# The up weights of the last two experts, issued in ScalarE's DMA queue instead of SyncE's

## What is computed

```python
hid = (jax.nn.silu(jnp.einsum('bld,edh->bleh', xf, w_gate[grp]))
       * jnp.einsum('bld,edh->bleh', xf, w_up[grp]))
y = y + jnp.einsum('bleh,ble,ehd->bld', hid, combine[:, :, grp], w_down[grp])
```

## Time and profile before

| what | value |
|---|---|
| time, median of 3 runs | 1054.71 us (1054.44 to 1054.72) |
| time of the profiled execution | 1053.88 us |
| its span, first to last instruction | 1052.1 us |
| TensorE busy | 1010.9 us, 96% |
| mean granted TensorE clock | 0.986 of full speed |
| HBM read and written | 169.16 MB, 12.60 MB |

### The profile page before, as it was taken

How to read it: one execution, slowest core, us unless ns; L and a number is a source line. 1 busy time by engine, 2 the same in 40 slices (tenths; PEclk the granted TensorE clock), 3 DMA queues, 4 the chain that set the end, 5 groups by cost and what they waited for, 6 DMA issues and landing times. The chain is left out here.

```text
span 1052.1 us, 20893 instructions
## 1 busy us (share of the span) xinstructions
PE 1010.9 (96%) x8969; PEld 719.1 (68%) x8969; DVE 575.6 (55%) x1114; ACT 312.1 (30%) x581; POOL 112.6 (11%) x109
## 2 busy tenths in 40 slices
PE   9999999999999999999999999999999999787897
PEld 8888888877787877878866567544566665544454
DVE  6577786768569478388364464429464322111114
ACT  3346354535244343343333033010110111000013
POOL 3422222000000000000200100000001222111110
PEclk9999999999999999999999999999999999988899
DMA  9232222331332242142212212165877999999976
GB/s 275 67 81 67 62 62 63 80 66 41 82 66 63 61 85 63 41 86 63 58 54 69 63 45 77 42 245 184 335 283 261 414 414 416 413 417 414 417 300 250
DMA packets 113007, 174.76 MB, mean 166 GB/s; under 512 B 9027, under 2 KB 87116, under 8 KB 104594
## 3 DMA queue, kind: packets, MB, share of 16 engines
q1 hardware_dynamic: 100050, 134.93, 37.4%
q10 hardware_dynamic: 7136, 27.33, 6.6%
q0 software_dynamic: 5728, 11.14, 4.0%
HBM read 169.16 MB, written 12.60 MB: 173 GB/s over the span
## 5 line engine op out<-in xcount | busy, mean ns | idle before, releaser
L829 PE MATMUL ps<-arena 128*128 128x256 f32 x1008 | 237.6, 385 | 0.0
L829 PEld LDWEIGHTS ps<-arena 128*128 128x128 f32 x1008 | 185.2, 190 | 27.3 <-issue 2.8
L1523 DVE TENSOR_TENSOR arena<-arena 128x256 f32<-128x256 f32 (+6 forms) x202 | 111.5, 594 | 46.4 <-ACT arena L1314 32.7
L859 PE MATMUL ps<-arena 128*128 128x264 f32 x400 | 124.0, 392 | 0.8 <-DVE gates L1655 0.8
L2513 PE MATMUL ps<-arena,gates 128*64 128x256 f32 (+1 forms) x1088 | 106.1, 352 | 16.4 <-DMA arena<-in_expert_w_up 16.0
L860 PE MATMUL ps<-arena 128*128 128x264 f32 x400 | 121.7, 386 | 0.0
L2513 PEld LDWEIGHTS ps<-arena,gates 128*64 128x64 f32 x1088 | 72.6, 143 | 56.4 <-DMA arena<-in_expert_w_up 25.5
L853 PE MATMUL ps<-yT,arena 128*128 128x512 f32 x192 | 84.8, 596 | 2.1 <-DVE gates L1655 1.4
L860 PEld LDWEIGHTS ps<-arena 128*128 128x128 f32 x400 | 76.0, 190 | 13.0
L859 PEld LDWEIGHTS ps<-arena 128*128 128x128 f32 x400 | 71.7, 190 | 13.1 <-issue 2.8
L2692 DVE COPY gates<-ps 128x1024 f32<-128x1024 f32 x15 | 18.4, 1225 | 102.0 <-PE ps L2494 102.0
(11 more groups left out here) (404 smaller groups left out, 1447.6 us busy)
## 6 DMA issues: line engine op xcount, KB each, us to landing
arena<-in_w_in SPq DMA_DIRECT2D x68, 512.0 KB, 4.0
arena<-in_expert_w_gate SPq DMA_DIRECT2D x27, 1024.0 KB
arena<-in_expert_w_up SPq DMA_DIRECT2D x27, 1024.0 KB
arena<-in_expert_w_down ACTq DMA_DIRECT2D x16, 1024.0 KB
arena<-in_w_branch SPq DMA_DIRECT2D x12, 512.0 KB, 4.2
arena<-in_expert_w_down SPq DMA_DIRECT2D x6, 1024.0 KB
C<-in_expert_w_gate SPq DMA_DIRECT2D x5, 1024.0 KB
gates<-in_expert_w_up SPq DMA_DIRECT2D x5, 1024.0 KB
```

The costliest lines, as they stand in the source:

```text
L829: mm = t.matmul(dst, wt[:, k, :], rhs[:, k, :], start=(k == 0), stop=(k == KH - 1))
L859: t.matmul(dst[:, 0:HALF], wt, uT[:, k, 0:HALF], start=(k == 0), stop=(k == KD - 1))
L1523: v.tensor_tensor(out_, a_, b2, op).then_inc(*q.did(name))
```

## The change

For `e` = 24 and 25, that is experts 30 and 31, SyncE issues only the gate weights behind `up(e)`. ScalarE issues their up weights in its own queue, behind `result(e)`. All other loads, their waits and the two late down loads of SyncE stay as they were. No computation changes.

```diff
@@ esync @@
                     sp.wait_ge(*up_made.of(e))
-                    load_up(sp, e % U, e + U)
+                    load_gate(sp, e % U, e + U)
+                    if e + U < NX - LATE:
+                        load_second(sp, e % U, e + U)
                 for e in range(NX - U - LATE, NX - U):
                     sp.wait_ge(*made.of(e))
                     load_down(sp, e % U, e + U)
@@ escalar @@
                     result(e)
                     if e + U < NX - LATE:
                         load_down(a, e % U, e + U)
+                    elif e + U < NX:
+                        load_second(a, e % U, e + U)
                     if e >= NX - 5 and e + 2 < NX:
                         sigmoid(e + 2)
```

## The result

The changed kernel takes 1059.15 us (median of 5 runs, 1058.74 to 1060.69) against 1054.71 us: 0.49% slower, ratio 1.0049 with a 95% interval of 1.0038 to 1.0059, that is 4.0 to 6.2 us. Run twice more, it gave 1.0063 (1.0050 to 1.0077) and 1.0047 (1.0033 to 1.0061) against the kernel before beside it.

A forecast was written before the change was run, and what follows sets the result against it. Loads were taken to pace the middle of the expert stage, TensorE its last 12 us. A later `up(30)` (3.9) plus its clock fall (2.2) made +6.1 us on the 1054.71 us median: 1060.8 us, range 1058.2 to 1062.5.

The forecast's parts named there:

- The place in the line: Up 30 stands behind ScalarE's backlog of down weights, so `up(30)` starts at 1017.5 instead of 1013.60 us: 3.9 us.
- Turns by packet: Queues alternate packet by packet, so up 30's 8 KB packets beside SyncE's 4 KB get two thirds: 3.9 us to load.
- The lag of the last DMA engine: The last engine works on ScalarE's down weights until about 1013.6 us, though the engines' mean is through before 1010.
- rival C: Not slower: ScalarE's line ends before 1008.7 us, the wait before `up(30)` goes: -1.0 us, 1053.7 us; 9%.
- The clock: After a wait of 4.9 us TensorE's clock falls and `up(30)` takes 1.4 to 3.0 us longer; 2.2 taken.
- The sum: Later start of `up(30)` plus its slow products: 3.9 + 2.2 = 6.1 us, giving 1060.8 us on the median.
- waits of `up(25)` and `up(27)` unchanged (3.3 and 3.1 us): Sign in the changed kernel's timeline: TensorE's waits before these two products stay at 3.3 and 3.1 us.
- The other items costed at nothing: SyncE's and ScalarE's issues, up 31's landing, the down weights of experts 30 and 31, GpSimd's scatters: no cost or gain.
- The rule I had set against my reading: Read strictly, the change is worth 7.9 us of SyncE's sequencer, which nobody waits for, plus the later issue's effect.

The follow-up runs named there:

- runs 7: The changed kernel itself, unaltered, timed again against the kernel before: 1060.39 us, ratio 1.0063.
- run 9: The changed kernel itself, unaltered, timed once more against the kernel before: 1059.28 us, ratio 1.0047.
- Experiments 1: Against the changed kernel, up weights of experts 30 and 31 go back to SyncE's queue, issued at the late moment: 1058.34 us, ratio 1.0035.
- experiments 2: Against the changed kernel, only expert 31's up weights are in ScalarE's queue, expert 30's back with SyncE: 1054.65 us, ratio 0.9997.
- experiment 3: Against the changed kernel, only expert 30's up weights are in ScalarE's queue, expert 31's back with SyncE: 1061.74 us, ratio 1.0068.
- experiment 6: The changed kernel with each of ScalarE's two up loads cut into two loads of 4 KB packets, same bytes: 1061.94 us, ratio 1.0072.
- experiment 8: The changed kernel, with TensorE awaiting expert 29's down weights, then making 15 matmuls on constants before `up(30)`: 1059.5 us, ratio 1.0044.
- Experiment 5: Against the changed kernel, ScalarE issues the two up loads early, right behind the sigmoids of experts 24 and 25: 1061.23 us, ratio 1.0059.

## Why the prediction was right

**The place in the line** held. `up(30)` starts 4.33 us later than before in the profiles; 0.55 of that is already there at `up(27)` (989.34 against 988.79), so 3.8 us are the change's, where 3.9 was forecast. That it agrees to 0.1 is luck: counted the same way, runs 7 and 9 give 3.5 and 5.5. Experiments 1 to 3 bear out each part: a place in SyncE's line is worth 2.8 us (1), expert 31 is not on the path (2), and what stands beside the load in the other line sets its length (3).

**Turns by packet** held, by experiment 6. **The lag of the last DMA engine**, which I could only estimate by counting 9.2 loads, held too: ScalarE's line moved next to nothing after 1010 us on the mean of the engines, and yet its last load landed at 1013.20 in experiment 8. The profile of before would have told it without an estimate. Its DMA view from 1012.5 to 1013 us still has one packet of q10, and the one from 1013 to 1013.6 has none. A load of ScalarE's line was thus unfinished until after 1012.5, where rival C needed the line's end before 1008.7. The rival "not slower" rested on the mean and fell with it.

**The clock** came out at +2.4, +2.4 and +1.8 us on `up(30)` in three profiles, where 1.4 to 3.0 was the bound and 2.2 the choice. My ground for it, that all waits of 2.74 us or more had the fall, was too strong: it is no rule, as the last section shows, and only for the longest waits (the ten of 4.08 us and more in the expert stages of all the profiles) did it hold throughout. And that the longer wait is nearer to the dearer case, by which I chose 2.2, has nothing to support it: in the profile of before the longest wait of the expert stage had one of the cheapest falls (5.01 us against 6.64 after 3.07),

```profile
920.41 5.01 PE L2513 MATMUL ps<-arena,gates 128*64 128x256 f32 x32 [3.56 <-DMA arena<-in_expert_w_up]
```

and in experiment 3 a wait of 7.07 us had a cheaper one (5.59) than the changed kernel's 4.90 (6.04). The 2.2 came out near by luck.

**The sum** was +6.1 us; the profiled execution has +6.5, the medians of the three measurements +4.4, +5.8 and +4.8. The profile's +6.5 is made of 3.8 for the place, 2.4 for the clock, the 0.55 from before `up(27)`, which no term had, and 0.3 less tail. The median is 1.7 us below the forecast, inside the range. The term most likely too large for the median is the clock's, since a wait of 3 us doesn't bring its fall every time (last section), though it did before `up(30)` in all three profiles of this kernel. That is argued; experiment 8 was to show it and its times didn't. The mean granted clocks of the single runs don't either: the changed kernel's first five runs took 1060.69 us at 0.991 and 1058.74 at 0.986.

**A sign that I gave wrongly:** "waits of `up(25)` and `up(27)` unchanged (3.3 and 3.1 us)". The wait before `up(27)` was 1.72 us. Its start hardly moved. The fall of the clock had moved to `up(25)` (6.66 us instead of 5.04), so that TensorE arrived later and waited less. The start of products that wait for a load is the load's; the length of the wait before them is not.

**The other items costed at nothing** held: the issues of ScalarE took 0.38 us, `up(31)` and the last down products had no wait for loads, and the tail followed to 0.3 us.

The rule I had set against my reading, that another issuer saves only sequencer time (the Trainium skill, DMA: Bandwidth & Descriptors, Issuing engines are not separate DMA queues), does not hold here as far as "only" goes. The transfers do interleave on the same engines, as it says, but what is moved to another queue changes its place and its share. Experiment 5 shows it best: issued no later than before but in the other queue, the two loads take away the wait before `up(30)` and put one of 5.07 us before `down(29)`, 6.7 us in all. Experiment 1 against the changed kernel points the same way (27.5 us from `up(27)` to `up(30)` instead of 28.6, 28.3 and 30.3), from a single profile.

No version here beats the kernel before; moving expert 31's load alone ties with it.

## What to carry to other kernels

Where two DMA queues are both backlogged, ask of a load that changes queues what stands ahead of it there, what stands beside it in the other queue, and how large both queues' packets are: in these runs the three set its landing, and the moment of issue mattered only through them. A load that is needed next has no place behind a backlog of loads that are needed later, and a queue that looks idle on the mean of the DMA engines may still have work on the last of them: look for its last packet, not for where its mean share falls. A wait of TensorE costs its own length and often a slow stretch behind it (here after waits as short as 2.06 us, and not after every one of 3 us); that stretch counts only where no later wait hides it.

## What the hardware showed that I had not expected

That the share of two backlogged queues can be set by the shape of the transfer: cutting a load's runs from 8 KB to 4 KB, same bytes and queue, took q10 from 0.41 MB beside 0.29 to 0.34 beside 0.37 in 2 us. And the clock's fall doesn't keep to one place: in the changed kernel `up(27)` took 3.67 us in two profiles and 6.55 in the third, and none of it reached the end, because the wait before `up(30)` absorbed it.

Nor does the length of a wait settle whether the clock falls. In the profile of experiment 1, whose kernel issues nothing differently from the one before until after 960 us, these waits passed without it (timeline, then windows with columns as in the earlier trace rows):

```profile
920.38 3.67 PE L2516 MATMUL ps<-arena,gates 128*64 128x256 f32 x32 [3.37 <-DMA arena<-in_expert_w_up]
...
937.32 3.67 PE L2516 MATMUL ps<-arena,gates 128*64 128x256 f32 x32 [3.14 <-DMA arena<-in_expert_w_up]
...
971.85 5.36 PE L2516 MATMUL ps<-arena,gates 128*64 128x256 f32 x32 [3.47 <-DMA arena<-in_expert_w_up]
```

```profile
920.30:924.10 3.80, 3.72 (x33) 2.33 (x34) 0.00 (x0) 0.00 (x1) 0.00 (x0) 1.00 1.03 422
```

After 3.37 and 3.14 us the products took 3.67 us, at a clock of 1.00 after the first; after 3.47 us they took 5.36. The changed kernel has such a case too: in run 9 the products behind a wait of 2.80 us (at 953.49) were not slow. In the kernel before, 2.74 us had been enough, and in the profiles of experiments 2 and 6 `up(26)` took 5.36 us after waits of only 2.11 and 2.06 us. What decides between them stays open here.
